# Output projection of a hybrid layer: gate spread once, banks emptied by a multiply, last chunk tile by tile

## What is computed

```
adaLN(c) -> shift, scale, gate            (per sequence: one for the prompt, 8 for the sample)
z = (RMSNorm_pre(x) * (1 + scale) + shift) @ W_in
attention branch (top-k sparse) and state-space branch, each times SiLU of its gate
mix = concat(branches)                    (1152 x 2048)
y = x + gate * RMSNorm_post(mix @ W_out)  RMSNorm_post(o) = g_post * o / sqrt(mean(o*o) + 1e-6)
```

## Time and profile before

| | |
|---|---|
| time, median of 3 runs | 2444.31 us (2441.04 to 2452.64) |
| profiled execution, its own time | 2446.5 us |
| its span | 2444.5 us |
| output projection in it | from 1978.25 us on, 466 us |
| TensorE (PE) busy | 2214.7 us, 91% of the span |
| PE weight load (PEld) | 1909.6 us, 78% |
| VectorE (DVE) | 1252.7 us, 51% |
| ScalarE (ACT) | 745.9 us, 31% |
| GpSimd (POOL) | 471.4 us, 19% |

### The profile page before, as it was taken

One profiled execution on the slowest core, in us unless ns is written; L12 is line 12 of the kernel. 1 busy time (PEld: TensorE's weight loads), 2 busy tenths in 40 slices (PEclk: granted clock), 3 DMA queues, 4 the chain that ended last, 5 costly groups with the idle time before them and its releaser, 6 DMA issues. The chain is left out here.

```text
span 2444.5 us, 33881 instructions
## 1 busy us (share of the span) xinstructions
PE 2214.7 (91%) x13056; PEld 1909.6 (78%) x13056; DVE 1252.7 (51%) x2264; ACT 745.9 (31%) x1338; POOL 471.4 (19%) x661
## 2 busy tenths in 40 slices
PE   4779999999999999999899998697769989998896
PEld 3469999889797999999779698595446868886774
DVE  3226433677595952355479795444525652113224
ACT  3221222222323233322232432432324532222231
POOL 0000432890000002033345365000000000003001
PEclk7889999999999999999999999697979999999997
DMA  7856456345453352677646343624211022225435
GB/s 274 307 163 144 136 156 173 101 108 132 114 142 85 99 193 74 152 232 214 191 128 181 108 132 95 184 73 137 68 49 49 18 74 74 77 76 182 131 93 177
DMA packets 432902, 323.58 MB, mean 132 GB/s; under 512 B 123209, under 2 KB 376689, under 8 KB 431465
## 3 DMA queue, kind: packets, MB, share of 16 engines
q1 hardware_dynamic: 423778, 310.57, 44.3%
q10 hardware_dynamic: 8976, 11.01, 1.3%
HBM read 263.48 MB, written 62.23 MB: 133 GB/s over the span
## 5 line engine op out<-in xcount | busy, mean ns | idle before, releaser
L1481 PE MATMUL ps_z<-h_hi_a,w_hi 128*128 128x384 f32 (+1 forms) x1408 | 488.3, 347 | 19.9 <-DVE h_lo_a L1093 18.5
L1483 PE MATMUL ps_z<-h_hi_a,w_lo 128*128 128x384 f32 (+1 forms) x1408 | 475.8, 338 | 0.0
L1482 PE MATMUL ps_z<-h_lo_a,w_hi 128*128 128x384 f32 (+1 forms) x1408 | 474.8, 337 | 0.0
L1151 DVE TENSOR_TENSOR w_lo<-w_raw,w_hi 128x1024 fp32r<-128x1024 f32 (+1 forms) x135 | 185.9, 1382 | 368.8 <-ACT w_hi L898 368.2
L1481 PEld LDWEIGHTS ps_z<-h_hi_a,w_hi 128*128 128x128 f32 (+1 forms) x1408 | 265.4, 189 | 51.3 <-issue 40.9
L1482 PEld LDWEIGHTS ps_z<-h_lo_a,w_hi 128*128 128x128 f32 (+1 forms) x1408 | 265.9, 189 | 1.2
L1483 PEld LDWEIGHTS ps_z<-h_hi_a,w_lo 128*128 128x128 f32 (+1 forms) x1408 | 265.2, 188 | 1.4
L898 ACT ACTIVATE w_hi<-w_raw 128x1024 fp32r<-128x1024 f32 (+1 forms) x180 | 185.9, 1052 | 226.4 <-PE ps_z L1483 221.5
L1481 PE MATMUL ps_z<-h_hi_b,w_hi 128*128 128x384 f32 (+1 forms) x720 | 249.8, 347 | 0.6 <-DVE w_lo L1151 0.4
L1483 PE MATMUL ps_z<-h_hi_b,w_lo 128*128 128x384 f32 (+1 forms) x720 | 242.5, 337 | 0.0
L1482 PE MATMUL ps_z<-h_lo_b,w_hi 128*128 128x384 f32 (+1 forms) x720 | 242.1, 336 | 0.0
(11 more groups left out here) (408 smaller groups left out, 3760.6 us busy)
## 6 DMA issues: line engine op xcount, KB each, us to landing
w_raw<-in_w_in SPq DMA_DIRECT2D x176, 512.0 KB, 4.0
wada<-in_w_ada SPq DMA_DIRECT2D x32, 1024.0 KB, 13.4
o_raw<-in_w_out SPq DMA_DIRECT2D x128, 256.0 KB, 3.0
wg<-in_w_ada SPq DMA_DIRECT2D x32, 512.0 KB, 6.2
zt<-z_sb SPq DMA_DIRECT2D x36, 384.0 KB, 4.6
zt<-z_sb SPq DMA_DIRECT2D x36, 192.0 KB, 3.5
x_add<-in_x_prompt SPq DMA_DIRECT2D x20, 256.0 KB, 3.2
out_y_prompt<-out_rows SPq DMA_DIRECT2D x10, 512.0 KB, 4.6
```

The costliest lines, as they stand in the source:

```text
L1151: V.tensor_tensor(w_lo[r][:, :, 0:m], w_raw[r][:, :, 0:m], w_hi[s][:, :, 0:m].bitcast(F32), ALU.subtract).then_inc(w_lo_ok, 1)
L1481: M(out, hi, H_HI[p][:, kk, cols], start=kk == 0, stop=False)
L1482: M(out, hi, H_LO[p][:, kk, cols], start=False, stop=False)
L1483: return M(out, lo, H_HI[p][:, kk, cols], start=False, stop=kk == KB - 1)
```

## The change

Only `project_out` is changed. In its own words, with line numbers of the kernel after:

- **The gate is spread once**, in chunk 0: eight matmuls of `sel` by `gpost` (`gate_unit`, two at each of blocks 11 to 14, into banks 5 to 7). ScalarE copies four of them to `gate` (the prompt's row, 128 x 2048) and four, the sample's, to row buffer 4 (`keep_gates`). POOL stores row buffer 4 to memory (`gs_out`), since tile 4 needs the buffer, and loads it back (`gs_in`) when tile 4 is out again.
- **Banks are emptied by a multiply**: at the end of a chunk ScalarE only squares, and VectorE multiplies each bank by the gate into the row buffer (`evict`). It waits for `gs_out` before tile 4's first, for the tile's stores before group 1's first, and for `gs_in` before tile 8's. There are eight banks, taken in turn, and TensorE waits for the bank of seven tiles before (`bank_free`).
- **A final** is one VectorE instruction for half a tile: row buffer times 1/rms plus x (`final`, 128 x 1024). Group 0's ten come one by one at blocks 1 to 10 of chunk 4. POOL no longer adds; it issues the loads of x by whole tiles (seven when group 0's last matmul is done, into slabs of the state-space and attention inputs that nothing reads any more, tiles 7 and 8 later), and group 0's stores.
- **The last chunk's weights** come beside chunk 6: `SPLIT` puts a block of chunk 7 after each block of chunk 6, in SP's loads, ScalarE's copies and VectorE's low parts. Fourteen blocks go to columns 0:512 or 512:640 of the mix arrays, which belong to tiles 0 to 4 and are read no more (`halves_of`); two use the usual buffers.
- **Chunk 7 goes tile by tile**: 48 matmuls of tile 5, then of tile 6, and so on. 1/rms, the multiply, the finals and the stores (on SP's queue) follow each tile; the multiply stands between the second and the third small step.

```diff
-        ps_o = [... f"ps_out{i}" ... for i in range(5)]
-        ps_g = [... f"ps_gt{i}" ... for i in range(2)]
+        banks = [... f"ps_out{i}" ... for i in range(8)]
+        SPLIT = [0]
+        for _m in range(LAST):
+            SPLIT += [_m + 1] if _m + 1 < LAST else []
+            SPLIT += [LAST + _m % KB] if _m >= LAST - KB and _m % KB < IN_SLABS else []
+        SPLIT += [LAST + KB - 2, LAST + KB - 1]
...
         def _(sp):
+                if in_slab(m):
+                    if m == LAST:
+                        sp.wait_ge(y_ok, 10)
+                    sp.dma_start(raw, wide(src, raw)).then_inc(slab_in[m - LAST], 16)
...
+            for m in SPLIT[2:]:
+                load(m)
+            for t in range(5, NT):
+                for h in range(2):
+                    store_half(sp, t, h)
...
         def _(pool):
-                    nc.gpsimd.tensor_tensor(part, part, x, ALU.add).then_inc(y_ok[n % 2], 1)
+            pool.wait_ge(g_kept, 2 * NOC)
+            pool.dma_start(scr["gate_dram"], rows[4][:]).then_inc(gs_out, 16)
+            pool.wait_ge(out_mm, tiles_before(1, 0))
+            for t in range(7):
+                load_x(pool, t)
+            for t in range(5):
+                for h in range(2):
+                    store_half(pool, t, h)
+            pool.wait_ge(y_out[4], 32)
+            pool.dma_start(rows[4][:], scr["gate_dram"]).then_inc(gs_in, 16)
+            for t in (7, 8):
+                pool.wait_ge(y_ok, 2 * (t - 2) + 2)
+                load_x(pool, t)
...
         def _(act):
-                    A(rows[i][:, bass.ds(c * OC, OC)], ps_o[i][:], ACT.Copy).then_inc(out_read, 1)
+            def keep_gates(u):
+                act.wait_ge(g_mm, u + 1)
+                dst = (gate if u < NOC else rows[4])[:, OC * (u % NOC):OC * (u % NOC) + OC]
+                A(dst, banks[5 + u % 3][:], ACT.Copy).then_inc(g_kept, 1)
...
         def _(dve):
-                V.scalar_tensor_tensor(part, part, stat[:, 4, i:i + 1], ps_g[...][:], ALU.mult, ALU.mult).then_inc(scaled, 1)
+            def evict(g, c, i):
+                dve.wait_ge(squared, n + 1)
...
+                if n == 4:
+                    dve.wait_ge(gs_out, 16)
+                if g == 1 and c == 0:
+                    dve.wait_ge(y_out[i], 32)
+                sample = OUT_GROUPS[g][0] + i == NT - 1
+                if sample and c == 0:
+                    dve.wait_ge(gs_in, 16)
+                V.tensor_tensor(rows[i][:, cols], bank_of(g, c, i)[:], (rows[4] if sample else gate)[:, cols], ALU.mult).then_inc(out_read, 1)
...
+            def final(t, h):
+                dve.wait_ge(x_in[t], 16)
+                dve.wait_ge(out_read, ...)
+                V.scalar_tensor_tensor(split, split, stat[:, 4, i:i + 1], x_tile(t)[:, 2 * h:2 * h + 2], ALU.mult, ALU.add).then_inc(y_ok, 1)
...
         def _(pe):
-                    for f in finals_at(g, c, kb):
-                        gates(0, f)
+            for i in range(4):
+                bank_free(1, NOC - 1, i)
+                for kb in range(KB):
+                    if i == 0:
+                        pe.wait_ge(w_lo_ok, turn_of_split(LAST + kb))
+                    ins = product(LAST + kb, i)
+                ins.then_inc(out_mm, 1)
```

More of the change, by code:

```diff
@@ L2484, in project_out @@
[L2484 to L2489, removed]
         HALF_D = D_MODEL // 2
+        GATE_AT = 5
+        UNIT_AT = 11
+        gpost = nc.alloc_sbuf_tensor_at("gpost", [P, HALF_D], F32R, offset=keep["maskb_base"])
         parts = rows[1]
@@ L2524, in x_piece @@
[L2524 to L2535, removed]
@@ L2538, in tiles_before, with step_of @@
-        def tiles_before(g, c):
[L2540 to L2556, removed]
+        def step_of(m):
+            return m // (NOC * KB), m // KB % NOC, m % KB
@@ L2569, in send @@
[L2569 to L2586, removed]
@@ L2601, in _ @@
+            for m in SPLIT[2:]:
[3 more added lines that the diff above has]
+                    store_half(sp, t, h)
+            for t in range(NT):
+                sp.wait_ge(y_out[t], 32)
         @block.gpsimd
@@ L2667, in _, with high @@
-            act.wait_ge(ssq_ready, 1)
-            high(0, 0, 0)
-            chunks(act, body)
-            for H in range(halves[1]):
-                store_half(act, 1, H)
+            def high(m):
+                raw, hi, _ = halves_of(m)
+                if in_slab(m):
+                    act.wait_ge(slab_in[m - LAST], 16)
+                else:
+                    act.wait_ge(w_in[m % 2], 16 * ((m if m < LAST else m - IN_SLABS) // 2 + 1))
+                    before = m - 2 if m < LAST else m - KB
+                    if before >= 0:
+                        used(act, before)
+                A(hi, raw, ACT.Copy).then_inc(w_hi_ok, 1)
@@ L2673, in _ @@
+            high(LAST + KB - 1)
+            for i in range(4):
+                squares(1, NOC - 1, i)
+                root(1, i)
         @block.vector
@@ L2826, in _, with product @@
-            chunks(pe, body)
-            for f in range(len(finals[1])):
-                gates(1, f)
+            def product(m, i):
+                g, c, kb = step_of(m)
+                mix_hi, mix_lo = MIX_HI[kb // NB], MIX_LO[kb // NB]
+                t = OUT_GROUPS[g][0] + i
+                cols = slice(P * t, P * t + P)
+                _, hi, lo = halves_of(m)
+                to = wide(bank_of(g, c, i)[:], hi)
+                M(to, mix_hi[:, kb % NB, cols], hi, start=kb == 0, stop=False)
+                M(to, mix_hi[:, kb % NB, cols], lo, start=False, stop=False)
+                return M(to, mix_lo[:, kb % NB, cols], hi, start=False, stop=kb == KB - 1)
```

387 lines of the change are left out of this document (199 added, 188 removed).

## The result

The changed kernel takes 2405.8 us, median of four runs (2403.7 to 2407.3), where the kernel before took 2443.2 beside it: a ratio of 0.984 (0.981 to 0.987). Its profiled execution took 2407.3 (span 2405.5), 39.2 less than that of before. The forecast was 2409, within its range, and the way it named, faster. But two of its terms were wrong by about 7 us each, in opposite directions.

A forecast was written before the change was run, and what follows sets the result against it. TensorE bounds the kernel up to the last matmul, then a 30.0 us tail. From 2446.5 us, 3.0 + 4.7 - 3.3 - 24.5 + 7.5 - 4.6 - 20.0 = -37.2 gave 2409, range 2399 to 2425.

The forecast's parts named there:

- the tail: After the last matmul starts: only one tile's work remains, 10.0 us in place of 30.0, so -20.0.
- chunks 2, 3, 6 and 7 at their price: These chunks lose nothing at their boundaries: -2.2 us for chunks 2 and 3, -2.8 for 6 and 7.
- the eight gate matmuls of chunk 0: Chunk 0: gate matmuls in pairs at four blocks cost 4 x 0.75 = +3.0 us.
- the root's stall: Start of chunk 4: table load and small steps delay the second block's low part, a stall of 2.9 us.
- Weights land in 3.0, and 5.4 would do.: Chunk 4: weight loads land soon enough not to stall PE; part of chunk 4's -24.5 us, to 48.2.
- Rival B: Chunk 4: seven x tiles posted at once delay a weight load 19 us, PE stands 12; 2421 us, chance 0.13.
- the reload's +7.5: Start of chunk 5: tile 8's multiply waits for the sample gate to return to row buffer 4, +7.5 us with clock.
- The first boundary: End of chunk 0: VectorE waits for POOL's store of row buffer 4, stall 2.9 and clock 1.8, +4.7 us.
- Rival C: POOL's queue moves one transfer at a time, PE stands 54 us at chunk 5's start; slower, 2457 us, chance 0.05.
- 1.8 us of lower clock behind each stall: After stalls at the first boundary, chunk 4 and chunk 5: a lower clock, read from chunk 5, loses 1.8 us.

The follow-up runs named there:

- by_block: The changed kernel with chunk 7 going block by block over the four tiles again, its weights still loaded beside chunk 6; ratio 0.989.
- sp_burst: The changed kernel with its seven x tiles posted on SP's queue, ahead of chunk 4's third weight block; ratio 0.988.
- deep: The changed kernel with 14 of chunk 4's 16 weight blocks loaded into four raw buffers in dead slab rows; ratio 0.984.
- spread_root: As spread, with group 0's root and small steps one block later; ratio 0.984.
- deep_defer: As deep, with x tiles 5 and 6 loaded only once chunk 4 is done; ratio 0.982.
- before_pool: The kernel before with group 0's x loads and y stores issued from POOL's queue, SP's queue carrying weights alone; ratio 0.999.
- best3: As best2, but group 0's finals, x loads and stores go by tiles 4, 0, 1, 2, 3, gate reload behind tile 2's stores; 2390.2 us, ratio 0.978.
- spread: The changed kernel with POOL's order altered: x tiles 0, 1 first, 2 to 4 between stores, 5 and 6 after the gate's reload; ratio 0.985.
- deep_defer_root: As deep_defer, with group 0's root and small steps one block later; ratio 0.982.
- best2: As best1, with group 0's finals one block later, at blocks 2 to 11; ratio 0.980.
- best1: As deep_defer_root, with the four raw weight buffers lasting through chunks 4 and 5 (30 blocks) and the sample's gate spread first; ratio 0.980.

## Why the forecast was right, and where not

The time was right for a half-wrong reason. What held: the tail (10.0 forecast, 9.4 measured; by_block shows that the order of tiles makes most of it), chunks 2, 3, 6 and 7 at their price, the eight gate matmuls of chunk 0, and the root's stall, in its place if not in its size (1.7 us for 2.9: the table load ran from 1.30 us into the chunk, right behind the last square and beside VectorE's last multiply and first numbers, and not after them).

**The step that failed is in chunk 4**: "Weights land in 3.0, and 5.4 would do." The 3.0 of the earlier trace rows is a median over the whole stage, mostly with little else under way. Within chunk 4 the kernel before had another:

```profile
o_raw<-in_w_out SPq DMA_DIRECT2D x16, 256.0 KB, 4.3
```

Those loads took 3.5 to 6.2 beside x quarters and stores, so the trace of before already had landings over 5.4. Beside the burst a load took 8.0, and chunk 4 cost 7.5 us more than forecast. Rival B named that place, but it made the load wait for all the burst, which sp_burst shows to be the case of one queue.

**The second is the reload's +7.5**, which did not come. The landing came near: 55.1 us after the start of chunk 4 by the working, 53.6 measured (2262.68 against 2209.09). But it was set against a chunk 4 of 48.2; a chunk of 55.7 hid it. And it came near for another reason. The last store's issue to landing, in the changed kernel (issued 41.7 us into chunk 4) and in deep (issued at 32.8):

```profile
out_y_prompt<-out_rows POOLq DMA_DIRECT2D x1, 512.0 KB, 4.2
out_y_prompt<-out_rows POOLq DMA_DIRECT2D x1, 512.0 KB, 13.8
```

In the changed kernel the queue had been worked off by then: late weights made the finals late, and with them the stores. Only deep, with a chunk 4 of 46.0, has the full queue that the working priced; there the reload landed at 51.9, and the wait is there. The two terms hang together: both come from 17.8 MB that have to go in chunk 4, and more than half of what deep wins at the weights it loses at the reload (chunks 4 and 5 together are 100.1 us in the changed kernel and 95.9 in deep). I priced them apart, as if a late chunk 4 would not pay for chunk 5, and was lucky that the errors met.

**The first boundary** was too dear: 4.7 forecast. POOL's store landed in 5.4 (6.9 taken from the gate's load), VectorE waited 1.7 and PE 1.0, and the clock stayed at 1.00 behind it:

```profile
gate_dram<-out_rows POOLq DMA_DIRECT2D x1, 1024.0 KB, 5.4
DVE out_rows L2718 <- DMA gate_dram<-out_rows: 1.7, 1, 1.7
```

Over the profiles with that wait chunk 1 lost 1.0 to 2.6.

**Rival C fell**: from POOL's first issue (2209.57) to the landing of the last store (2254.98) 12.6 MB took 45.4 us, 277 GB/s, where it wanted under 150. VectorE was busy for 23.4 of these 45.4 us, nearly all of it with operations of two tensor inputs, and POOL issued the seven tiles of x 0.74 us apart. Nothing was seen to be shut out. The Trainium skill (SBUF — State Buffer, "Who interferes with whom") says that VectorE operations in a two-port mode shut POOL's descriptors out and that tensor_tensor does not. This case agrees as far as it goes; no run put operations of the shutting kind beside POOL's transfers. The Trainium skill (DMA: Bandwidth & Descriptors, "Queues, rings and completion order") also says that each engine alternates between queues by packet. The trace agrees, with a weight load 5 us late beside POOL's queue against 16 in one queue with the same bytes.

## What to carry to other kernels

A transfer's landing time holds for the traffic under which it was measured: where a change puts megabytes beside a stream of small loads, look for landings under the like traffic (here up to 2.8 times the quiet time), and compare them with what the stream's buffers cover (blocks ahead times the time of a block). Where several waits hang on the same bytes, price them as one: spread_root, deep, deep_defer and before_pool each removed a stall that came back, in part or whole, at another wait. In best3 four raw buffers in dead rows, the tile whose buffer is wanted back finished first, and a few moves in the order (root and finals a block later, two tiles of x a chunk later, the sample's gate spread first) took 15 us more off the projection with no operation less; not each of them was measured alone.

## What was not expected of the hardware

- Two queues share: a load of 0.25 MB, 2.9 us alone, took 4.0 to 8.0 beside 1 MB tiles in POOL's queue (the change, spread), and up to 7.5 even where single tiles went between stores (spread). Beside 0.5 MB stores alone it took 2.9 to 5.1 (the change, spread, sp_burst).
- POOL's queue was not slow: its 1 MB store landed in 5.4 us, where SP's 1 MB load took 6.9, and an issue took POOL 0.5 to 0.8 us.
- An issue on SP's queue waits when much stands in it: the seven 1 MB tiles of sp_burst took SP 0.6 us each at first and 2.7 at the end.
- I took 1.8 us of lower clock behind each stall. PE idle at one go for 1.0 us (chunk 1 of the change), 2.1 (deep_defer_root's chunk 4) or 3.0 (best2's chunk 5) left the chunk at 1.00, while 2.0 us (best1's chunk 4) and 2.6 (chunk 5 of deep_defer_root) were followed by 0.96 and 4.5 (deep's chunk 5) by 0.97. So the length of the idle time alone does not tell, and what does was not tried.
